# Page numbers loaded once during the input projection, and products that wait for a norm by halves, in a hybrid decoder step on one Trainium2 core

## What is computed

```
h = x + 1/2 * g1 * SwiGLU_1(mod(rms(x)))              # feed-forward 1, behind norm 1
n = mod(rms(h)); z = n @ W_in                          # input projection, behind the mixer's norm
  A: conv GLU -> depthwise conv (31) -> LayerNorm -> swish -> W_conv_out
  B: indexer scores, top-k keys, sparse attention -> W_attn_o
h = h + g2 * W_out( sigmoid(gate_A)*A + sigmoid(gate_B)*B )
h = h + 1/2 * g3 * SwiGLU_2(mod(rms(h)))               # feed-forward 2, behind norm 2
y = RMSNorm_final(h)
```

## Time and profile before

| | |
|---|---|
| median of 3 runs | 2641.59 us (2638.42 to 2644.48) |
| profiled execution | 2641.7 us, span 2639.9 us |
| PE busy | 2485.7 us, 94% of the span |
| DVE, ACT, POOL busy | 1401.2, 662.7, 1458.6 us |
| chain that ended last | PE 82%, DVE 6%, issue 4%, SPq 3%, ACT 3% |
| mean granted clock of PE | 0.970 |

### The profile page before, as it was taken

The page is one execution under the profiler, slowest core; times in us unless marked ns, Lnnn a source line. Parts: engine busy times, 40 slices in busy tenths (PEclk is TensorE's granted clock), DMA queues, the critical chain, the costliest instruction groups (busy, mean ns, idle before and its releaser), DMA issues.

```text
span 2639.9 us, 44639 instructions
## 1 busy us (share of the span) xinstructions
PE 2485.7 (94%) x16038; PEld 2307.2 (87%) x16038; DVE 1401.2 (53%) x2619; ACT 662.7 (25%) x1238; POOL 1458.6 (55%) x1234
## 2 busy tenths in 40 slices
PE   5999999999998888899999779999899999999997
PEld 3899999999997756699998446789799999999997
DVE  5543334434446638799998445462564444444444
ACT  3311011111112323335544457310511111111113
POOL 1276666666665325536999020124057777777774
PEclk8999999999999879999999969999999999999999
DMA  8422222222221532231224600334011111111112
GB/s 288 120 68 77 72 67 68 79 79 79 73 79 53 151 74 77 75 102 49 79 92 145 220 11 1 98 98 146 1 33 48 49 53 50 53 49 48 48 48 82
DMA packets 243128, 209.99 MB, mean 80 GB/s; under 512 B 14687, under 2 KB 207315, under 8 KB 241993
## 3 DMA queue, kind: packets, MB, share of 16 engines
q1 hardware_dynamic: 232844, 181.70, 22.9%
q10 hardware_dynamic: 10181, 26.90, 3.2%
HBM read 173.03 MB, written 28.94 MB: 77 GB/s over the span
## 4 chain that ended last, share of the span: by engine, by line
PE 82%; DVE 6%; issue 4%; SPq 3%; ACT 3%; POOL 1%; DMA 0%; ACTq 0%; DVEq 0%; POOLq 0%
PE main L763 11%; PE main L764 10%; PE main L765 10%; PE main L295 7%; PE main L296 7%; PE main L297 7%; PE main L864 5%; PE main L865 5%; PE main L866 5%; SPq L1925 2%; DVE pick L1742 2%; PE main L2144 2%; PE main L2161 1%; PE aux L2172 1%; PE aux L763 1%
## 5 line engine op out<-in xcount | busy, mean ns | idle before, releaser
L684 POOL TENSOR_TENSOR blo<-raw,bhi 128x512 fp32r<-128x512 f32 x424 | 553.5, 1306 | 34.0
L682 POOL CAST bhi<-raw 128x512 fp32r<-128x512 f32 x424 | 264.7, 624 | 544.8 <-PE main L866 311.4
L763 PE MATMUL main<-nhi,bhi 128*128 128x352 f32 x1312 | 429.1, 327 | 17.9 <-issue 10.8
L764 PE MATMUL main<-nlo,bhi 128*128 128x352 f32 x1312 | 423.0, 322 | 0.0
L765 PE MATMUL main<-nhi,blo 128*128 128x352 f32 x1312 | 422.8, 322 | 0.0
L295 PE MATMUL main<-nhi,whi 128*128 128x352 f32 x1032 | 340.3, 330 | 1.0 <-DVE pick_s L1730 0.5
L297 PE MATMUL main<-nhi,wlo 128*128 128x352 f32 x1032 | 334.1, 324 | 0.0
L296 PE MATMUL main<-nlo,whi 128*128 128x352 f32 x1032 | 334.1, 324 | 0.0
L1100 DVE SCALAR_TENSOR_TENSOR h<-main,ada,h 128x352 f32<-128x352 f32 (+1 forms) x448 | 251.9, 570 | 84.5 <-PE main L866 84.5
L864 PE MATMUL main<-hid_hi,bhi 128*128 128x352 f32 x896 | 292.1, 326 | 4.7 <-DVE h L1100 2.8
L282 POOL CAST whi<-raw 128x1024 fp32r<-128x1024 f32 x51 | 56.4, 1106 | 422.0 <-issue 234.6
(11 more groups left out here) (379 smaller groups left out, 5130.7 us busy)
## 6 DMA issues: line engine op xcount, KB each, us to landing
raw<-in_w_gate SPq DMA_DIRECT2D x44, 512.0 KB, 4.1
raw<-in_w_up SPq DMA_DIRECT2D x44, 512.0 KB, 3.9
ada_part<-in_w_ada SPq DMA_DIRECT2D x44, 512.0 KB, 5.0
raw<-in_w_down SPq DMA_DIRECT2D x44, 512.0 KB, 3.9
raw<-in_w_in SPq DMA_DIRECT2D x40, 512.0 KB, 3.9
ada_raw<-in_w_ada SPq DMA_DIRECT2D x7, 2048.0 KB, 12.0
gate_d<-zraw ACTq DMA_DIRECT2D x16, 528.0 KB, 2.7
gates<-gate_d SPq DMA_DIRECT2D x16, 528.0 KB, 4.7
```

Of the source, the lines that this page charges most:

```text
L682: pool.tensor_copy(bhi[:, slot], src).then_inc(sg.block_hi.sem, 1)
L684: pool.tensor_tensor(blo[:, slot], src, bhi[:, slot].bitcast(F32), ALU.subtract)\
L763: pe.matmul(out, bhi[:, slot, w], hi(c), start=start and c == 0, stop=False, skip_group_check=True)
L764: pe.matmul(out, bhi[:, slot, w], lo(c), start=False, stop=False, skip_group_check=True)
```

## The change

Two things. (1) m1_sp reads each of the 16 page numbers once more, behind the load of one of the last 16 tiles of the input projection (L = 25 to 40), and keeps it in a register of SP (page_of). pages() of m2_sp uses these registers; it loads nothing. The loads for the indexer keys stay. (2) ready takes the half. pe_first calls it ahead of either half's unit at m == 0. m1_pe calls it with half L: for L = 0 the first four rows need half 0 only, and the hook "middle" waits for half 1 ahead of the fifth row; L = 1 waits for half 1, which the product before it has already waited for.

```diff
--- before.py
+++ after.py
@@ -535,8 +535,8 @@
                 dve.tensor_tensor(nlo[:, c4s[half], tcs(t)], tmp[:, c4s[half], :],
                                   nhi[:, c4s[half], tcs(t)].bitcast(F32), ALU.subtract).then_inc(s["lo"], 1)
 
-            def ready(pe, t):
-                norm_wait(pe, q, "lo", 2 * t + 2)
+            def ready(pe, t, half=1):
+                norm_wait(pe, q, "lo", 2 * t + half + 1)
             return {"gather": gather, "total": total, "square_act": square_act, "square_more": square_more, "square_pool": square_pool, "square_dve": square_dve,
                     "root": root, "inverse": inverse,
                     "scale": scale, "affine": affine, "low": low, "ready": ready}
@@ -774,9 +774,9 @@
                 pe.wait_ge(*banks_free)
                 for t in range(NTC):
                     for m in range(2):
-                        if m == 0:
-                            nrm["ready"](pe, t)
                         for half in range(2):
+                            if m == 0:
+                                nrm["ready"](pe, t, half)
                             sg.block_ready.wait(pe, 2 * m + half + 1)
                             pe_unit(pe, 2 * m + half, X(half, t), bank(3 * m + t), half == 0, half == 1)
                         nrm["pe_between"](pe, 2 * t + m)
@@ -1238,6 +1238,8 @@
             n = 2 * (6 * (L - Z_Q - 1) + 2 * t + half)
             return range(n, n + 2) if L > Z_Q and n < len(PIECES) else range(0)
 
+        page_of = []
+
         def m1_sp(sp):
             for L in range(3):
                 first.block_ready.wait(sp, NBLOCKS - (4, 2, 0)[L])
@@ -1269,6 +1271,10 @@
                          allow_slow_non_contiguous=True).then_inc(wr_in, 16)
             for L in range(Z_Q + 1, NZ):
                 load_tile(sp, T_Z + L, L % RING, cols(w_in, ZCOL[L]))
+                n = L - (NZ - 2 * NSEQ)
+                if n >= 0:
+                    page_of.append(sp.value_load(a["page_table"][n // 2:n // 2 + 1, n % 2:n % 2 + 1], min_val=0,
+                                                 max_val=L0["cache_k"].shape[0] - 1))
 
         def m1_pool(pool):
             def post(L):
@@ -1346,8 +1352,9 @@
         def m1_pe(pe):
             for t in range(NTC):
                 for L in range(2):
-                    norm_m["ready"](pe, t)
-                    z_product(pe, L, T_Z + L, L % RING, 3 * L, L % 2, 72 if L == 0 else P, ts=(t,))
+                    norm_m["ready"](pe, t, L)
+                    z_product(pe, L, T_Z + L, L % RING, 3 * L, L % 2, 72 if L == 0 else P, ts=(t,),
+                              middle=(lambda t: norm_m["ready"](pe, t)) if L == 0 else None)
                     if (L, t) == (0, 0):
                         norm_m["total"](pe, 2)
             for L in range(2, Z_Q):
@@ -1922,9 +1929,7 @@
                 load_tile(sp, T_MIX + m, (T_MIX + m) % RING, mix_load(m))
             def pages(b, cache, dst, done):
                 for pg in range(2):
-                    page = sp.value_load(a["page_table"][b:b + 1, pg:pg + 1], min_val=0,
-                                         max_val=cache.shape[0] - 1)
-                    sp.dma_start(dst[:, pg, :], cache[bass.ds(page, 1)].rearrange("o p h d -> (o p) (h d)"))\
+                    sp.dma_start(dst[:, pg, :], cache[bass.ds(page_of[2 * b + pg], 1)].rearrange("o p h d -> (o p) (h d)"))\
                         .then_inc(done, 16)
 
             def keys_of(b):
```

## The result

The changed kernel takes 2625.77 us (median of 6, 2623.35 to 2632.81) against 2643.03 us for the kernel before (median of 6, 2638.42 to 2652.51): 17.3 us less, ratio 0.994 with a 95% interval of 0.9924 to 0.9957. A later set gave 2624.66 against 2647.63 (median of 13) and 0.993 (0.9904 to 0.9956), so the two medians for the kernel before are themselves 4.6 us apart. The forecast was 2623.8, with a range of 2616 to 2630. The time fell as forecast and lies in the range, but the terms of the sum fared differently.

What follows compares the result with a forecast made beforehand. TensorE bounds the chain, waiting 12.19 us for value pages behind SP's page-number loads and for whole norm chunks. Terms -13.0 - 3.3 - 1.6 + 0 = -17.9 us take 2641.7 to 2623.8 us, range 2616 to 2630.

Steps and rivals of the forecast that it cites:

- Term A: Before the attention: early page numbers end TensorE's 12.19 us wait for value pages, VectorE's select comes earlier; -13.0 us.
- R3: Rival: another wait, such as key stores or a late key page, replaces SP's; 2636.8 us, chance 0.04.
- Term B: Norm 1: TensorE starts after the first low half, at 61.18 in place of 64.45; -3.3 us, bounds 0 and 3.3.
- Added waits and the pairs of loads: Waits riding on matmuls, and 16 register-load pairs in the input projection inside SP's wait for POOL's split; 0 us taken.
- R4: Rival: slower, register loads between weight DMAs make SP late with the projection's weight tiles; 2647 us, chance 0.02.
- Term C: Mixer's norm: TensorE starts chunk 2 after its first half, 884.86 in place of 886.46; -1.6 us, bounds 0 and 1.6.
- Term D: Norm 2, before the second feed-forward: chunk 1 ends earlier but chunk 2 still waits; 0 us, bounds 0 and -1.9.
- R1: Rival: the early starts of the norms are taken back, leaving Term A alone; 2628.7 us, chance 0.13.
- The clock: Attention: TensorE's low-clock stretch (1540 to 1564) taken as unchanged, 0 us; 6 us more would go if it stayed high.
- R2: Rival: TensorE's clock stays at 2.4 GHz into the attention, saving 6 us more; 2617.8 us, chance 0.12.

Runs made afterwards that it cites:

- key pages only: Changed kernel with only key pages addressed by registers loaded early, each value page loading its number before its transfer again; 2628.03 us, ratio 0.9939.
- value pages only: Changed kernel with only value pages addressed by registers loaded early, each key page loading its number before its transfer; 2625.3 us, ratio 0.9938.

## Why the prediction was right, and where it was not

The forecast of 2623.8 lies 2.0 us below the median, inside its range. By the table's means, two profiles of the changed kernel against three of the kernel before:

**Term A, forecast -13.0:** 96.1 to 82.4, so -13.7. The mechanism held in its main steps: pages issued by 1479.7 (forecast 1479.8), no wait at the value products (so R3 is out too), and the select tied to the scaling. In the first profile the shift was 11.4 us (95.1 to 83.7), 1.6 less than forecast: the delay by the stores of keys, for which 1.5 us were allowed, did come. On the other side the idle time I started from was the smallest of three. One step was mis-sized without harm: issued closely, the value pages took 6.1 to 9.8 us to land in place of 2.7 to 5.6, and still all were there some 20 us before the first value product. One sentence failed: that "SP's other page numbers (16 for keys, 8 of them during the last tiles of the projection) cost nothing now". No wait of TensorE names them in the first profile, but they stand ahead of the value pages on SP's queue; with those loads alone gone the stretch is 8.7 us shorter (96.1 to 87.4). In the second and third profile of the kernel before TensorE waits for key pages too (timeline of PE, second profile):

```profile
1474.71 1.81 PE L2033 MATMUL main<-cst,kpg 128*128 128x128 f32 x8 [1.93 <-DMA kpg<-in_cache_k]
```

**Term B, forecast -3.3:** 10.6 to 7.1, -3.5, as worked out. **Added waits and the pairs of loads, forecast 0:** the stretch of the projection is as long with the early loads as without (571.4 and 571.1 against 571.3 us), so SP's wait for POOL's split did cover them; R4 is out.

**Term C, forecast -1.6:** the stretch from the first kiw product to the end of the projection fell from 575.2 to 571.3, -3.9, so this term was mis-sized. Between the starts of chunk 0 and chunk 2 it is -1.6 (23.1 us to 21.5) as forecast. Another 0.9 lies right behind, to the first L1361 product (56.8 us before, 55.9 after): after the shorter pause fewer of the 336 products there run at the low level (18 or 19 before, 13 or 14 after). So the term left out what the shorter pause does to the clock. The remaining 1.4 us lie further on in the projection, and most of it is the first profile of the kernel before: from the first L1361 product to the end it took 496.7 us there and 494.5 and 494.8 in the two others, against 494.0 and 493.8 in the changed kernel. All ten profiles with the halves have 570.3 to 571.9 for the whole stretch and all four without them 574.1 to 576.6, so the halves are worth at least 2.2 us of it. What they do behind the first L1361 product stays open.

**Term D, forecast 0, bounds 0 and -1.9:** measured +2.8, outside the bounds. The step that failed is that I followed the freed 2 us along TensorE, VectorE and ScalarE, and not to POOL, for whose ring TensorE's products free a block. That rival R1 spoke of early starts being "taken back" was too weak: here an early start cost more than it gave. The excess over term C (2.3 us) and the loss in norm 2 (2.8) nearly cancel, which is why the sum came out; that is luck.

**The clock, forecast 0 (R2 -6):** the out stage's end comes 343.7 us behind the first L2144 product, and 343.1 in the mean before. The low stretch moved with the attention (it ends 28 to 29 us behind the first L2144 product in the changed kernel's two profiles, 24 to 29 in the three before; the stretch to out's end is 1 us longer in the profiles where it ends at 28 or 29), and the unit of 3.87 us is there again, at the low level (timeline of PE, windows):

```profile
1548.21 1.65 PE L2149 MATMUL main<-ka,qa 64*128 64x384 f32 x4
1552.08 0.92 PE L2149 MATMUL main<-ka,qa 64*128 64x384 f32 x4
```

```profile
1550.00:1552.00 2.00, 2.00 (x12) 1.09 (x11) 1.84 (x7) 0.98 (x3) 0.00 (x0) 0.50 0.00 0
1552.00:1554.00 2.00, 2.00 (x16) 1.03 (x15) 0.91 (x5) 1.41 (x5) 0.00 (x0) 1.00 0.00 0
```

R2 is out: the clock's low stretch is no shorter without the 12 us pause. One reading in the forecast was loose: not all of the work after 1524 was sustained. In the kernel before TensorE was busy for 1.42 of the 4 us from 1536 and for 2.79 of the 4 from 1548; from 1540 to 1548, though, it was busy throughout, at 0.50. Sum of the measured stretches, the start left out: -13.7 - 3.5 - 3.9 + 2.8 + 0.6 (attention and out) = -17.7 us, and the timed medians differ by 17.3 in the first set and by 23.0 in the later one.

## What to carry to other kernels

When a change lets an engine go on sooner, follow everything that engine releases, the buffers it frees included: here an earlier product let POOL start beside VectorE's critical sums, and 2 us gained became 2.8 lost, which one longer wait on POOL undid. A register load in front of a DMA costs its queue, not the wait that names it: count all loads that stand ahead of the late transfer, also those for which no one is seen to wait. And take two or three profiles of the kernel before, if you can, before a term is built on one idle time; this one read 12.2, 15.2 and 14.3 us.

## What the runs showed of the hardware

The same sum of 128x1408 elements on VectorE took 1.62 us alone and 1.92 or 2.71 us while POOL split blocks; the low half in norm 1 took 2.60 or 1.63 us in the same way from one execution to the next. Holding POOL back brought 1.62 us back, so the overlap does it. Of POOL's two steps it is the subtraction (L684): beside a cast alone (L682) VectorE's operation kept its 1.62 or 1.63 us (at 1912.34 in the kernel before, at 1897.12 in the changed one), and in none of the 14 profiles did a single operation of this shape take over 1.8 us without a two-input operation of POOL's beside it. Not every such overlap lengthens it: one at 1917.04 in the changed kernel kept 1.63 us, while the subtraction that began at 1917.27 took 2.54. Alone that subtraction takes 1.29 us, beside the sums it took 2.55. What the two share, no run here shows. By the Trainium skill, page "Advanced Engine Details and Errata", section "GPSIMD Details", the Pool engine shares a read and a write interface with VectorE and conflicts with instructions that have two SBUF inputs, which these sums are. The durations beside POOL's subtractions agree with that rule; the casts beside them cost VectorE nothing.

A value page landed in a median of 2.7 us when issued every 2.7 us and in 9.1 us (at most 9.8) when 16 were issued in 12.9. The stores of keys beside them made ScalarE wait 0.5 to 2.5 us, and 5.4 us where they met head on. The view of the tile vpg in the changed kernel has the landings:

```profile
DMA to landing us min/median/max: 6.1/9.1/9.8
```

TensorE's clock: behind an idle time of 5.2 to 5.6 us in the mixer's norm 18 or 19 products ran at 1.2 GHz, behind 4.7 to 4.9 us 13 or 14. In two profiles (key pages only, value pages only) the idle time came in two parts of 2.4 and 1.6 us, only 2 products were slow, and the first L1361 product came 75.2 us behind the first kiw product, against 77.2 to 78.1 in the other kernels with halves; yet the stretch to the end of the projection took 571.5 and 570.3 us, against 571.1 to 571.9 in the others.

The start differs by up to 12 us between executions with nothing changed there. The last L427 addition, which the rows of w_ada release through TensorE, came between 52.3 and 64.7 us; in the changed kernel's first profile at 62.41, in its second at 53.99. The spread of a kernel's times is of the same size, and an effect of 3 us shows in a stretch and hardly in a median of six. That the start makes that spread is not shown, since only one execution of each set was profiled.
